# First attention's value matmuls as three float32r products of split operands, two pieces into the next pair

## What is computed

```python
# layer 1 ("phase A"): chunked attention, 32 heads of 128
q, k, v, g = split(rms_norm(x) @ a_w_in)             # 2048 x 4*4096
p = softmax(q k^T * scale + rel_bias, masked)         # per head, 256 x 256
x = x + ((p @ v) * silu(g)) @ a_w_out                 # 4096 x 2048
# layer 2 ("phase B"): the same shape with forgetting attention
k_s, v_s = split(rms_norm(x) @ kv_w)                  # 2048 x 2*4096
logf = log_sigmoid(h_kv @ f_w + f_b)                  # f_w is 2048 x 32
q, g = split(rms_norm(x) @ b_w_in)
x = x + ((p @ v_s) * silu(g)) @ b_w_out
```

## Time and profile before

| | us |
|---|---|
| median of 3 runs | 2668.5 (2668.45 to 2671.25) |
| the profiled execution, its own time | 2673.9 |
| its span | 2671.8 |
| TensorE busy, in the span | 2638.3 |
| VectorE busy | 1860.7 |
| ScalarE busy | 1380.4 |

### The profile page before, as it was taken

One profiled execution on the slowest core, in us unless ns is written; L12 is line 12 of the kernel. 1 busy time (PEld: TensorE's weight loads), 2 busy tenths in 40 slices (PEclk: granted clock), 3 DMA queues, 4 the chain that ended last, 5 costly groups with the idle time before them and its releaser, 6 DMA issues.

```text
span 2671.8 us, 45699 instructions
## 1 busy us (share of the span) xinstructions
PE 2638.3 (99%) x16797; PEld 2370.5 (89%) x16797; DVE 1860.7 (70%) x2804; ACT 1380.4 (52%) x2124; POOL 135.4 (5%) x141
## 2 busy tenths in 40 slices
PE   8999999999999999999999999999999999999998
PEld 7888888888888888888888888888999899999887
DVE  7666666666665586666666666765889996689976
ACT  6444444444454464444444444544574674465664
POOL 0000000000000000101011010000000000000000
PEclk9999999999999999999999999999999999999999
DMA  7766666666656556666676666665555665566663
GB/s 226 213 192 210 195 201 201 195 209 197 205 173 198 188 163 200 202 194 207 196 209 191 198 203 195 200 192 188 179 175 173 185 191 174 166 191 186 207 212 127
DMA packets 513658, 514.76 MB, mean 193 GB/s; under 512 B 26922, under 2 KB 502466, under 8 KB 513282
## 3 DMA queue, kind: packets, MB, share of 16 engines
q1 hardware_dynamic: 490260, 488.01, 59.6%
q10 hardware_dynamic: 23296, 25.36, 3.2%
HBM read 489.93 MB, written 21.53 MB: 191 GB/s over the span
## 4 chain that ended last, share of the span: by engine, by line
PE 83%; DVE 10%; ACT 3%; DMA 2%; issue 2%; ACTq 0%; SPq 0%; DVEq 0%
PE proj L1360 33%; PE proj L1363 16%; PE proj L1375 9%; PE proj L1379 4%; PE proj L1548 4%; PE proj L1549 4%; PE proj L1550 4%; DVE scratch L2350 2%; DVE w_both L2191 2%; PE proj L1742 2%; DMA scratch<-probabilities 1%; PE ps_s L1453 1%; PE proj L1744 1%; ACT w_both L977 1%; DVE w_both L1841 1%
## 5 line engine op out<-in xcount | busy, mean ns | idle before, releaser
L1360 PE MATMUL proj<-operand,w_both 128*128 128x512 f32 x3968 | 1252.9, 397 | 3.4 <-DVE w_both L1841 2.7
L1841 DVE TENSOR_TENSOR w_both<-w_raw,w_both 128x1024 fp32r<-128x1024 f32 x644 | 797.6, 1241 | 626.3 <-ACT w_both L746 625.3
L746 ACT ACTIVATE w_both<-w_raw 128x1024 fp32r<-128x1024 f32 x644 | 678.1, 1058 | 832.7 <-PE proj L1363 636.3
L1363 PEld LDWEIGHTS proj<-operand,w_both 128*128 128x128 f32 x3968 | 746.2, 188 | 176.2
L1363 PE MATMUL proj<-operand,w_both 128*128 128x256 f32 x3968 | 780.5, 278 | 0.0
L1360 PEld LDWEIGHTS proj<-operand,w_both 128*128 128x128 f32 x3968 | 604.8, 189 | 4.4 <-DVE w_both L1841 3.3
L1548 PE MATMUL proj<-operand,w_both 128*128 128x272 f32 (+2 forms) x1540 | 445.9, 290 | 6.4 <-DVE w_both L2191 6.1
L1549 PE MATMUL proj<-operand,w_both 128*128 128x272 f32 (+2 forms) x1540 | 441.1, 286 | 0.0
L1550 PE MATMUL proj<-operand,w_both 128*128 128x272 f32 (+2 forms) x1540 | 440.9, 286 | 0.0
L2191 DVE TENSOR_TENSOR w_both<-w_raw,w_both 128x1024 fp32r<-128x1024 f32 x226 | 274.1, 1218 | 111.2 <-ACT w_both L977 110.5
L1375 PE MATMUL proj<-w_both,operand 128*128 128x512 f32 x1024 | 321.7, 395 | 0.0
(11 more groups left out here) (373 smaller groups left out, 2169.2 us busy)
## 6 DMA issues: line engine op xcount, KB each, us to landing
w_raw<-in_a_w_in_dram SPq DMA_DIRECT2D x256, 512.0 KB, 3.7
w_raw<-in_w_in_dram SPq DMA_DIRECT2D x160, 512.0 KB, 3.7
w_raw<-in_b_w_in_dram SPq DMA_DIRECT2D x128, 512.0 KB, 3.8
w_raw<-in_kv_w_dram SPq DMA_DIRECT2D x128, 512.0 KB, 4.1
w_raw<-in_a_w_out_dram SPq DMA_DIRECT2D x64, 512.0 KB, 4.4
w_raw<-in_b_w_out_dram SPq DMA_DIRECT2D x64, 512.0 KB, 3.7
w_raw<-in_w_out_dram SPq DMA_DIRECT2D x64, 512.0 KB, 3.6
probabilities<-scratch ACTq DMA_DIRECT2D x32, 384.0 KB, 2.5
```

Source lines behind the costliest of these rows:

```text
L746: act.activation(w_hi[:, s], w_raw[:, s], ACT.Copy).then_inc(hi_ready, 1)
L1360: pe.matmul(proj[:, 2 * bank + t, :], w_hi[:, s, kk, t * P:(t + 1) * P], rhs[:, k, :], start=first and k == 0, stop=False)
L1363: m = pe.matmul(proj[:, 2 * bank + t, 0:S], w_lo[:, s, kk, t * P:(t + 1) * P], rhs[:, k, 0:S], start=False, stop=last and end)
L1841: dve.tensor_tensor(w_lo[:, s], w_raw[:, s], w_hi[:, s].bitcast(F32), ALU.subtract).then_inc(pieces_split, 1)
```

## The change

The 256-column value matmul (L1453) is replaced by three float32r matmuls of split operands: `v_hi` by `p_hi`, `v_hi` by `p_lo`, `v_lo` by `p_hi`. The 128-column one stays in float32. ScalarE makes the high parts (one instruction for `v_hi`, two for `p_hi`), VectorE the low parts (one and two). `values(n)` moves from the end of pair n into the k unit of pair n + 1, ahead of that unit's piece 2. The two halves of the probability split stand behind the first split of the next pair, on ScalarE and on VectorE, and `gate_heads` behind the third one. `take_scaled` of q waits for `p_stored` in place of `p_landed`. The split parts take the place of tables that only the second block uses, and `v_tok` shares memory with `sumsq`. The load of `f_w` moves from SyncE's queue to ScalarE's. The diff, without the lines that only rename `qk_hi` and `qk_split` to `parts_hi` and `parts_split` and those that move the tables:

```diff
@@ -192,7 +196,11 @@
         x_res = sb("x_res", [P, KT, T])
-        scratch = sb("scratch", [P, 18152])
+        scratch = sb("scratch", [P, TABLES_AT])
+        with nc.sbuf_tensor("value_parts", [P, TABLE_FLOATS], F32R) as value_parts:
+            v_hi, v_lo = (value_parts[:, n * S:(n + 1) * S].rearrange("p (h d) -> p h d", h=2) for n in range(2))
+            p_hi, p_lo = (value_parts[:, (n + 1) * 2 * S:(n + 2) * 2 * S].rearrange("p (h s) -> p h s", h=2) for n in range(2))
+        tables = sb("tables", [P, TABLE_FLOATS])
         consts = sb("consts", [P, 2 * P])
@@ -224,9 +232,9 @@
         p_keys = one.take(4, 6, 32)
-        v_tok = one.take(2, S)
         tanh_g = one.take(2, S)
         sumsq = one.take(2, S)
+        v_tok = sumsq
@@ -564,9 +572,6 @@
                 load_pair(phase, PAIRS - 1, True)
-                if phase == "A":
-                    sp.wait_ge(og_split, 8)
-                    sp.dma_start(fw, io["f_w"].rearrange("(k p) n -> p k n", p=P)).then_inc(consts_in, 16)
                 with sp.Fori(1, OUT_N) as j:
@@ -821,6 +826,13 @@
+            def probabilities_hi(n):
+                act.wait_ge(p_landed, 64 * n + 64)
+                for h in range(2):
+                    m = act.activation(p_hi[:, h, :].rearrange("p (c a j) -> p c a j", c=2, a=4),
+                                       p_keys[:, :, 3 * h:3 * h + 2, :].rearrange("p a c j -> p c a j"), ACT.Copy)
+                m.then_inc(parts_hi, 1)
+
             def pair(phase, i, last, first=False):
@@ -828,17 +840,19 @@
                     split_hi(unit + 2, s)
+                    if s == 0 and not first:
+                        probabilities_hi(n - 1)
                     if first and phase == "A" and s == 2:
                         root_of(0)
                 copy_half(unit + 1, output + 1, 1)
                 act.wait_ge(scaled, 3 * n + 1)
-                act.activation(q_hi, q_t[:, :, P:S], ACT.Copy).then_inc(qk_hi, 1)
+                act.activation(q_hi, q_t[:, :, P:S], ACT.Copy).then_inc(parts_hi, 1)
...
                         act.wait_ge(scaled, 3 * n + 2)
-                        act.activation(k_hi, k_t, ACT.Copy).then_inc(qk_hi, 1)
+                        act.activation(k_hi, k_t, ACT.Copy).then_inc(parts_hi, 1)
                 act.wait_ge(proj_free, output + 4)
@@ -847,6 +861,8 @@
                 split_hi(unit + 4, 0)
+                act.wait_ge(proj_free, output + 5)
+                act.activation(v_hi, v_tok[:, :, 0:P], ACT.Copy).then_inc(parts_hi, 1)
                 if last:
@@ -919,6 +935,11 @@
                     split_hi(unit + 1 + c // 4, c % 4)
+                    if c == 1:
+                        probabilities_hi(pair0[phase] + PAIRS - 1)
+                if phase == "A":
+                    act.wait_ge(og_split, 8)
+                    act.dma_start(fw, io["f_w"].rearrange("(k p) n -> p k n", p=P)).then_inc(consts_in, 16)
@@ -1423,13 +1444,17 @@
-                multiply(unit + 1, 1, other, chunk_wait=first_wait if first else None)
+                def values_before(s):
+                    if s == 2:
+                        values(n - 1)
+
+                multiply(unit + 1, 1, other, chunk_wait=first_wait if first else values_before)
                 if first and phase == "A":
...
-                pe.wait_ge(qk_split, 2 * n + 2)
+                pe.wait_ge(parts_split, 4 * n + 2)
                 pe.wait_ge(og_done, n + 1)
@@ -1443,14 +1468,16 @@
                     multiply(unit + 4, 0, h_q)
-                    values(n)
             def values(n):
                 pe.wait_ge(p_landed, 64 * n + 64)
+                pe.wait_ge(parts_split, 4 * n + 4)
                 for h in range(2):
-                    first = p_keys[:, :, 3 * h:3 * h + 2, :].rearrange("p a c j -> p c a j")
+                    pe.matmul(ps_s[:, h, 0:S], v_hi[:, h, :], p_hi[:, h, :], start=True, stop=False)
+                    pe.matmul(ps_s[:, h, 0:S], v_hi[:, h, :], p_lo[:, h, :], start=False, stop=False)
+                    pe.matmul(ps_s[:, h, 0:S], v_lo[:, h, :], p_hi[:, h, :], start=False, stop=False)
+                for h in range(2):
                     second = p_keys[:, :, 3 * h + 2, :]
-                    pe.matmul(ps_s[:, h, 0:S].rearrange("p (c a j) -> p c a j", c=2, a=4), v_tok[:, h, 0:P], first, start=True, stop=False)
                     m = pe.matmul(ps_s[:, h, P:S].rearrange("p (a j) -> p a j", a=4), v_tok[:, h, P:S], second, start=False, stop=True)
@@ -1923,6 +1950,14 @@
+            def probabilities_lo(n):
+                dve.wait_ge(parts_hi, 4 * n + 4)
+                for h in range(2):
+                    m = dve.tensor_tensor(p_lo[:, h, :].rearrange("p (c a j) -> p c a j", c=2, a=4),
+                                          p_keys[:, :, 3 * h:3 * h + 2, :].rearrange("p a c j -> p c a j"),
+                                          p_hi[:, h, :].bitcast(F32).rearrange("p (c a j) -> p c a j", c=2, a=4), ALU.subtract)
+                m.then_inc(parts_split, 1)
+
             def pair(phase, i, last, first=False):
@@ -1930,20 +1965,24 @@
                     split_lo(unit + 2, s)
+                    if s == 0 and not first:
+                        probabilities_lo(n - 1)
+                    if s == 2 and not first:
+                        gate_heads(n - 1, 2 * i - 2)
                     if first and phase == "A" and s == 2:
...
                 take_scaled(output + 1, 1, k_t)
-                dve.wait_ge(qk_hi, 2 * n + 1)
-                dve.tensor_tensor(q_lo, q_t[:, :, P:S], q_hi.bitcast(F32), ALU.subtract).then_inc(qk_split, 1)
+                dve.wait_ge(parts_hi, 4 * n + 1)
+                dve.tensor_tensor(q_lo, q_t[:, :, P:S], q_hi.bitcast(F32), ALU.subtract).then_inc(parts_split, 1)
                 for s in range(PIECES):
                     split_lo(unit + 3, s)
                     if s == 1:
-                        dve.wait_ge(qk_hi, 2 * n + 2)
-                        dve.tensor_tensor(k_lo, k_t, k_hi.bitcast(F32), ALU.subtract).then_inc(qk_split, 1)
+                        dve.wait_ge(parts_hi, 4 * n + 2)
+                        dve.tensor_tensor(k_lo, k_t, k_hi.bitcast(F32), ALU.subtract).then_inc(parts_split, 1)
@@ -1960,6 +1999,8 @@
                 split_lo(unit + 4, 1)
+                dve.wait_ge(parts_hi, 4 * n + 3)
+                dve.tensor_tensor(v_lo, v_tok[:, :, 0:P], v_hi.bitcast(F32), ALU.subtract).then_inc(parts_split, 1)
                 dve.wait_ge(exp_done, 4 * n + 4)
@@ -1987,9 +2028,8 @@
                         split_lo(unit + 5, s)
-                    dve.wait_ge(p_landed, 64 * n + 64)
+                    dve.wait_ge(p_stored, 16 * n + 16)
                     take_scaled(output + 4, 0, q_t, scale=SCALE)
-                    gate_heads(n, 2 * i)
@@ -2099,6 +2139,8 @@
                         gated_lo(r, c + 3)
+                    if c == 2:
+                        probabilities_lo(pair0[phase] + PAIRS - 1)
                     if c == 3:
```

More of the change, by code:

```diff
@@ L66 @@
 O_OUT, LAYER_OUTPUTS = 20, 28
+TABLES_AT = 16648
+TABLE_FLOATS = 1536
 def last_piece(unit):
@@ L287, in build_program @@
         tanh_2 = [rc, spare.take(CT, T)]
-        two.at = max(attention_only, two.at)
+        two = Region(tables)
         sinks = two.take(DEPTH, HEADS_2)
@@ L364, in build_program @@
         scaled = sem("scaled")
-        qk_hi = sem("qk_hi")
-        qk_split = sem("qk_split")
+        parts_hi = sem("parts_hi")
+        parts_split = sem("parts_split")
         h_hi = sem("h_hi")
```

## The result

The changed kernel takes **2700.1 us** (median of 4 runs, 2696.5 to 2700.4) against 2668.5 us (2668.4 to 2671.3): 1.0111 times the time of before, 95% interval 1.0099 to 1.0123, or 32 us more. The profiled execution took 2699.9, its span is 2696.9.

A forecast was written before the change was run, and what follows sets the result against it. TensorE bounds the kernel, busy 2638.3 of 2671.8 us. Gains of -13.1 and costs of +9.3, +15.2, +3.8, +5.5, +1.7 give +22.4, 2696.3 profiled; median 5.4 lower, half the landings' 4.3 returned: 2693, range 2679 to 2706.

The forecast's parts named there:

- Products: TensorE's value matmuls: three float32r products replacing the float32 one save 0.15 us for each of 32 pairs, -4.8 us.
- Landings: Value matmuls on TensorE no longer wait for the probabilities to land, five waits before: -4.3 us.
- f_w: Phase A's output projection: f_w's load on ScalarE's queue ends the late weight pieces and their low clock, -4.0 us.
- Phase A's pairs: Ahead of piece 2, TensorE waits for the probabilities' low part, 0.62 us late 15 times: +9.3 us.
- Phase B's pairs: Same wait, take_scaled slowed by GpSimd: 1.17 us late in 13 pairs, 1.90 in two; +15.2 and +3.8 us.
- Phase ends: Low part stands behind the second gated_lo at each phase's end; TensorE 2.75 us late in both phases, +5.5 us.
- Low clock: Lower clock after a phase-end standstill, counted once for the two: +1.7 us; twice or never is in the range.
- Rival 2: Phase B: GpSimd is out of the way and take_scaled takes 0.69 us; 2683 us, chance 0.13.
- Rival 3: VectorE's two probability subtractions are dearer, 0.75 us more in 30 pairs, +22 us; 2715 us, chance 0.08.
- Rival 1: Split parts come in time in the pairs, leaving gains and phase ends, -5.9 us; about 2663 us, chance 0.07.

The follow-up runs named there:

- experiment 3: Changed kernel with the value matmuls ahead of piece 3 of the next pair's unit in place of piece 2; 2668.1 us.
- experiment 4: Changed kernel with the probability splits ahead of the next pair's first weight split on ScalarE and VectorE, values still ahead of piece 2; 2672.8 us.
- 5: Changed kernel with two more subtractions, into memory nobody reads, ahead of the two that make the probabilities' low part; 2721.9 us.
- 7: Changed kernel with the loop's values ahead of piece 3 and pair 15's ahead of piece 1 of the projection's second unit; 2659.9 us.
- experiment 10: Kernel before, float32 values moved ahead of the next pair's piece 3, pair 15's into the projection's second unit, f_w load on ScalarE's queue; 2664.7 us.
- 1: Kernel before with only the load of f_w moved from SyncE's to ScalarE's queue; 2667.4 us.
- experiment 2: Kernel before with float32 values moved ahead of the next pair's piece 2, gate_heads behind the third split, f_w load on ScalarE's queue; 2664.5 us.
- experiment 8: Changed kernel with the load of f_w back on SyncE's queue; 2700.1 us.
- 6: Changed kernel without GpSimd's addition of the causal mask in phase B, so its output is another; 2687.0 us.
- 9: Changed kernel with values ahead of piece 3, pair 15's in the projection's second unit, and f_w's load back on SyncE's queue; 2664.3 us.

## Why the prediction was right, and by how much each term

The forecast was 2693, in 2679 to 2706; measured 2700.1. Its mechanism is the one that the trace and experiments 3, 4 and 5 show: TensorE reaches the values before VectorE has made the low part, and the loss comes from the order, not from the work. The terms, against the two profiled executions:

- **Products, -4.8.** 0.146 a pair in the stretches, -4.7; 7 against 10 gave 4.4 to 4.9. The Trainium skill (FP8 and Floating Point Precision, TensorE Precision Notes) counts four passes for true float32; the estimate from that, 0.24 a pair and -7.5, is not what the runs show.
- **Landings, -4.3.** 5.0 in this profiled execution, but 2.9 between the medians of 1 and 2. The half that the prediction took back was about right.
- **f_w, -4.0.** Right in the sum: 4.0 between the stretches of before and of experiments 1 and 2, -3.5 in the medians of 1. But the prediction credits the move with it, and in the changed kernel the move isn't needed: by 8 nearly all of it is gained with f_w on SyncE's queue too, since the new wait, a unit ahead of the late pieces, lets them arrive.
- **Phase A's pairs, +9.3.** 9.8, or 0.65 a pair for 0.62.
- **Phase B's pairs, +19.0.** 21.9, the term that was furthest off. The usual pairs are as worked out (1.11 and 0.1, for 1.17); three instead of two pairs are longer, and the low clock followed one of them, 1.6.
- **Phase ends, +5.5.** 2.85 each, 5.7, both in the trace.
- **Low clock, +1.7.** 1.5 outside the pairs, but its size is luck: the prediction put it behind an end wait, and in this execution it followed neither; it stood at the start of phase B. (The other one is in phase B's pairs.)

The measured terms sum to +25.2, and the spans differ by 25.1 (2671.8 to 2696.9); the own times differ by 26.0 where the forecast had 22.4. So of the 7 us of the median 2.8 are in the terms, as much as phase B's pairs alone were off; 0.9 is start and end outside the span (2.1 before, 3.0 after), and 3.5 are in the step from the profiled execution to the median: the prediction took off 5.4, by which the profiled execution of before was slower than its median, and gave 2.2 back, while the profiled execution after lay 0.2 below its median. The landings explain part of the 5.4. Part of it is chance in four runs: the 2668.5 of before beside the change is the lowest of its four medians (2669.6 to 2670.9 in the others, 61 runs).

Rival 2, phase B like phase A, fell; by 6 it would have needed GpSimd's addition out of the way. Rival 3, dearer subtractions, fell: L1956 takes 0.42 at the mean for an operand in runs of 32. Rival 1 came true only in 3, 4, 7 and 9, where the order was made to allow it. The prediction puts its time at 2663, without giving half of the landings back as the forecast does; with that it is 2665, and experiment 3 measured 2668.1.

What stays open: why the granted clock falls behind one standstill and not behind the same one in another execution. At the start of phase B, behind a wait of 1.1 us that all of these kernels have, it fell in the kernel after and in 3, 4, 6 and 7, and not in 1, 2 and 10. In the kernel before and in 5, 8 and 9 it had already fallen in phase A's projection, some 160 us ahead, and did not fall there again. Each has one profiled execution, so this is no rule.

## What to carry to other kernels

When work is put between two steps of a ring of buffers, don't ask whether the engines have time but count the chain from the event that frees the slot: here 0.20 + 1.09 + 1.14 + 0.75 us against a piece of 2.79. If it doesn't fit, a later piece costs nothing (experiment 3), and the short step ahead of the long one little (experiment 4, 4.6 us more). When one edit takes a stall away and another puts a new one ahead of it, the old one may be gone by the new one alone: the sum for both edits can be right (-4.0 and +2.75 here) while the first edit by itself gains nothing in that kernel (experiment 8) and its full price in one without the new stall (experiments 1 and 9).

## What was not expected of the hardware

- The same standstill of TensorE (2.75 us late, at the end of a phase) was followed by a granted clock of 1.00 in the kernel after and of 0.79 in experiments 3 and 8, that is, by 0 or 1.7 us more. The window around it in the kernel after, and the two elsewhere in which the clock did fall:

```profile
788.00:796.00 8.00, 5.72 (x36) 5.18 (x37) 7.71 (x10) 5.17 (x6) 0.00 (x0) 1.00 0.58 197
962.00:970.00 8.00, 6.91 (x31) 5.51 (x30) 7.93 (x17) 7.97 (x19) 0.00 (x0) 0.79 0.25 80
1660.00:1668.00 8.00, 6.20 (x31) 5.49 (x30) 3.42 (x4) 1.06 (x1) 0.53 (x1) 0.79 0.54 163
```

- The spread of the kernel before, 5.9 us over 31 runs, shrank to 1.6 over 9 in experiment 2 and 1.0 over 11 in experiment 10, when TensorE no longer stood directly behind the landing of a DMA or behind the late pieces. It isn't the landings alone that can make it: experiment 3, with no landing wait but with the two end waits, has 5.0 over 11.
